# A two-block transformer layer: projections from three float32r matmuls on halves to one plain float32 matmul, and weights laid out in DRAM slot by slot

## The chip, the cores and the metric

The kernel runs on one core of one Trainium2 chip. The metric is the device time of one execution in microseconds (us). TensorE (PE in the profile, with its weight loads as PEld), VectorE (DVE), ScalarE (ACT) and GpSimd (POOL) each have their own instruction stream; SyncE (SP) here only issues DMAs. The streams meet in semaphores, written out by hand.

## The reference, cut to what matters

256 tokens of width 2048 pass through two blocks, all in float32. What the projections compute is plain matrix products with large weights:

```python
mod = c_act @ ada_w + ada_b                      # six vectors of 2048
h = rmsnorm(x, norm1_g) * (1 + sc1) + sh1
z = h @ w_in                                     # q, kc, vc, ks, vs, kw, vw, gates, lx, ly, ga, gb
o_a = nsa_attention(q, kc, vc, ks, vs, kw, vw, gates, ...)   # compressed, selected, window
o_b = gelu(ly) * rg_lru(causal_dwconv(lx), ...)
y = (sigmoid(ga) * (o_a @ proj_a) + sigmoid(gb) * (o_b @ proj_b)) @ w_out
x = x + g1 * y
gate, val = split(h2 @ ffn_up)                   # width 6144 each
x = x + g2 * ((gelu(causal_dwconv(gate)) * val) @ ffn_down)
# second block: another w_in, sliding window attention, s5_ssm, w_glu, w_ssm_proj, w_out
```

## The kernel before, in words

Activations lie transposed: features on the 128 partitions, the 256 tokens along the free axis. The weights are read once. SP walks a fixed list of **slots**, each a load of 1 MB into one of `RAW = 5` buffers `wraw[:, z % RAW, :]` of 2048 float32 a partition. A weight slot is 512 rows by 512 columns of a matrix, taken as four runs of 512 elements (2 KB) a partition. An "ada" slot is 128 rows of `ada_w` transposed (8 KB in one run a partition); VectorE multiplies it by the activated `c` and sums (L1051), which gives one column of `mod`. SP reloads a buffer when its last user is done: `ada_done` for an ada slot, `pe_units` for a weight slot.

A weight slot holds two **units** of 1024 elements a partition, and there are 809 units, in groups (`groups()`): 8 units for a group of 512 output columns of a 2048-row matrix, 12 or 4 for others. Three modes: "T" (weights stationary, 128x128, the activations of 256 tokens moving; all but 25 units), "N" and "TN" (the value projections, activations stationary), and one unit "GATES".

Products are made from halves. A float32 number is cut into a float32r part and the rest. For each unit u, ScalarE copies the raw weights to float32r, `whi` (`split_act`, L1069), and VectorE subtracts it from the raw ones, `wlo`, over the raw buffer (`split_dve`, L1074). Both run `LEAD = 5` units ahead of TensorE, with `HI = 6` buffers `whi`. Activations are cut the same way by `split()` (L308: a cast and a subtraction) into pairs `_hi`, `_lo`. TensorE then issues, for each 128x128 block of weights, three float32r matmuls (L1525): whi by x_hi, whi by x_lo, wlo by x_hi. A T unit is 8 blocks, so 24 matmuls. Groups accumulate in two PSUM buffers (`pairs`, four rows of 256 tokens) in turn.

All engines walk the same order, `walk`: unit by unit, and after each unit some steps of **jobs**. A job is a generator, such as `evac` (read a finished group out of PSUM), `compress`, `nsa` (one of four key-value groups of the first attention; 27 steps), `lru`, `attention2`, `ssm` (eight, 17 steps each) or `norm1`, `norm2` and `last_norms`. Each job is spread over a stretch of units, so that TensorE does a unit, then its part of the next steps, waiting there where an engine has not delivered. The small matmuls of the jobs are plain float32 (into `bank`). The four `nsa` jobs lie in q(1), q(2), q(3), and the last in lx(0) and ly(0), 8 units each for the first three and 16 for the last. Each `ssm` job lies in 10 units of ga2, pa2 and gs2. Because the splits run 5 units ahead and in each engine's own stream, a `whi` that waits for its load or for a free buffer also holds up every ScalarE step behind it.

The start (`prologue`) is four blocks: 8 ada slots, then the norm of four chunks of `h1` (L335, L340, and the split at L310 and L312), then the splits of units 2b and 2b+1. TensorE may run units 2b and 2b+1 once block b of `h1` is there.

The result of the first block is kept in `res`; it goes to DRAM and comes back (`spilled`, `xf_back`, `x_back`) when its place is used for other data.

Of the kernel before, what the change touches and what calls it, by code (L numbers as in the profile page):

```python
# [6 lines left out]
F32 = mybir.dt.float32  # L7
F32R = mybir.dt.float32r
ACT = mybir.ActivationFunctionType
ALU = mybir.AluOpType  # L10
# [12 lines left out]
RAW = 5  # L23
HI = 6
LEAD = 5
# [76 lines left out]
def build_program(nc, ctx, xT, vecs, cvec, W, small, outT):  # L102
# [9 lines left out]
    def put_pair(name, at, n):  # L112
        return put(name + "_hi", at, [P, n, T], F32R), put(name + "_lo", at + n * 1024, [P, n, T], F32R)

# [3 lines left out]
    z0, z1, z2, rM, rW = 0, 32 * K, 64 * K, 96 * K, 112 * K  # L118
    rWh = rW + RAW * 8 * K
    rC = rWh + HI * 4 * K  # L120
    rT = rC + 8 * K
    rS = rT + 8 * K
    h1, m1 = put_pair("h1", z0, DC), put_pair("m1", z0, DC)
    oa, ob = put_pair("oa", z1, DC), put_pair("ob", z2, DC)
    h2, h3, m2 = put_pair("h2", z2, DC), put_pair("h3", z2, DC), put_pair("m2", z2, DC)
    hid = put_pair("hid", z0, 24)
    res = put("res", rM, [P, DC, T])
    wraw = put("wraw", rW, [P, RAW, 2048])
    wlo = put("wlo", rW, [P, RAW, 2, 1024], F32R)
    whi = put("whi", rWh, [P, HI, 1024], F32R)  # L130
# [3 lines left out]

    k2 = put("k2", z2, [P, 2, 4, T])
# [22 lines left out]
    u_2 = put("u_2", z1, [P, 8, T])  # L158
    q_2 = put("q_2", z1 + 8 * K, [P, 8, T])
    ag_2 = put("ag_2", z1 + 16 * K, [P, 8, T])  # L160
    k_2 = put("k_2", z1 + 24 * K, [P, 2, T])
    v_2 = put("v_2", z1 + 28 * K, [P, 2, T])
    rs2 = put("rs2", z1 + 30 * K, [P, 2, T])
    z_2 = put("z_2", z0, [P, 8, T])
    at_ = put_pair("at", z0 + 8 * K, 8)
    gs_2 = put("gs_2", z0 + 8 * K, [P, DC, T])
    y_2 = put("y_2", z1 + 24 * K, [P, 8, T])
    ys = put_pair("ys", z2, 8)
    sg = (put("sg_hi", z1, [P, 8, T], F32R), put("sg_lo", z1 + 24 * K, [P, 8, T], F32R))
    mg2 = put("mg2", z1 + 8 * K, [P, DC, T])  # L170
# [6 lines left out]
    ph = put("ph", z0 + 24 * K, [P, 4, 32, 16])  # L177
# [35 lines left out]
    def sem(name):  # L213
# [3 lines left out]
    hi_ready, lo_ready, pe_units, ada_done = sem("hi_ready"), sem("lo_ready"), sem("pe_units"), sem("ada_done")  # L217
# [3 lines left out]
    wcmp_in, wgate_in, x_back, spilled, ssm_in, xf_back = (sem("wcmp_in"), sem("wgate_in"), sem("x_back"),  # L221
                                                           sem("xf_spilled"), sem("ssm_in"), sem("xf_back"))
# [5 lines left out]
    X = {"h1": h1, "m1": m1, "h2": h2, "h3": h3, "m2": m2, "oa": oa, "ob": ob, "hid0": hid, "hid1": hid, "at": at_,  # L228
         "ys": ys, "sg": sg}
    block = ctx.enter_context(nc.Block())  # L230

    GR, of = groups()
    U0, U1 = [], []
    at = 0
    for gr in GR:
        U0.append(at)
        at += gr.units
        U1.append(at)
    N_UNITS = at
    SLOTS, HEAD = [], []  # L240
    unit_slot = {}
    behind = {}
    for g, gr in enumerate(GR):
        for s in range(gr.slots):
            per = gr.units // gr.slots
            if g == 0:
                HEAD.append(range(len(SLOTS), len(SLOTS) + 8))
                SLOTS += [("ada", col + c) for c in range(4 * s, 4 * s + 4) for col in (16, 0)]
            for n in range(per):
                unit_slot[U0[g] + s * per + n] = (len(SLOTS), n)  # L250
            SLOTS.append(("w", g, s, U0[g] + (s + 1) * per))
            for col in gr.ada.get(s, ()):
                behind.setdefault(U0[g] + (s + 1) * per - 1, []).append(len(SLOTS))
                SLOTS.append(("ada", col))
    N_ADA = 0
    ada_no = {}
    for z, slot in enumerate(SLOTS):
        if slot[0] == "ada":
            ada_no[z] = N_ADA
            N_ADA += 1  # L260
    where = []
    for gr in GR:
        where += [(gr, n) for n in range(gr.units)]
# [44 lines left out]
    def split(dst, at, n, src):  # L308
        hi, lo = dst
        ve.tensor_copy(hi[:, at:at + n, :], src)  # L310
        ve.drain()
        return ve.tensor_tensor(lo[:, at:at + n, :], src, hi[:, at:at + n, :].bitcast(F32), ALU.subtract)  # L312

# [15 lines left out]
    def normed(j, name, dst, c, r, gain, shift=None):  # L329

        me, ins = j.me, None
        if me == "dve":
            tt = (t1, t2)[c // 4 % 2]
            for n in range(4):
                ve.scalar_tensor_tensor(out=tt[:, n, :], in0=res[:, c + n, :], scalar=gain[:, c + n:c + n + 1], in1=r,  # L335
                                        op0=ALU.mult, op1=ALU.mult)
            ve.drain()
            if shift is not None:
                for n in range(4):
                    ve.tensor_scalar(tt[:, n, :], tt[:, n, :], mod[:, shift + c + n:shift + c + n + 1], None, ALU.add)  # L340
                ve.drain()
            ins = split(dst, c, 4, tt[:, :, :])
        j.ready[name].append(j.give("to_pe", "dve", ins))
# [69 lines left out]
    def nsa(j, i):  # L413
# [116 lines left out]
        for hd in range(4):  # L530
# [42 lines left out]
            if me == "dve":  # L573
                ins = split(oa, i * 4 + hd, 1, bank[3][:, 0:1, :])
                ve.drain()
# [3 lines left out]
    def lru(j, i):  # L579
# [59 lines left out]
        if me == "dve":  # L639
            ve.tensor_tensor(lr[:, :, :], lr[:, :, :], t2[:, :, :], ALU.mult)  # L640
            ve.drain()
            ins = split(ob, i * 4, 4, lr[:, :, :])
# [48 lines left out]
    def attention2(j, pair, e):  # L691
# [60 lines left out]
        for hd in range(4):  # L752
# [37 lines left out]
            if hd % 2:  # L790
                c = g * 2 + hd // 2
                if me == "dve":
                    j.eng.wait_ge(*evacuated("ag2", c // 4))
                if me == "dve":
                    ve.tensor_tensor(t1[:, 0:1, :], bank[3][:, 0:1, :], ag_2[:, c:c + 1, :], ALU.mult)
                    ve.drain()
                    split(at_, c, 1, t1[:, 0:1, :])
                    ve.drain()
# [20 lines left out]
    def ssm_tables(j):  # L819
# [4 lines left out]
        if me == "dve":  # L824
            j.eng.wait_ge(spilled, 16)
            ins = ve.drain()
        yield from j.hand("to_act", "dve", "act", ins)
# [233 lines left out]
    def width(u):  # L1061
        return 768 if where[u][0].mode == "GATES" else 1024

    def split_act(act, u):
        (z, half), r, w = unit_slot[u], u % HI, width(u)
        act.wait_ge(w_loaded[z % RAW], 16 * (z // RAW + 1))
        if u >= HI:
            act.wait_ge(pe_units, u - HI + 1)
        sc.activation(whi[:, r, 0:w], wraw[:, z % RAW, 1024 * half:1024 * half + w], ACT.Copy).then_inc(hi_ready, 1)  # L1069

    def split_dve(dve, u):
        (z, half), r, w = unit_slot[u], u % HI, width(u)
        dve.wait_ge(hi_ready, u + 1)
        ve.tensor_tensor(wlo[:, z % RAW, half, 0:w], wraw[:, z % RAW, 1024 * half:1024 * half + w],  # L1074
                         whi[:, r, 0:w].bitcast(F32), ALU.subtract).then_inc(lo_ready, 1)
        for z in behind.get(u, ()):
            ada(dve, z)

    def split_unit(j, u):
        if j.me == "act":  # L1080
            split_act(j.eng, u)
        if j.me == "dve":
            split_dve(j.eng, u)

    FIRST = 8

    def prologue(j):
# [17 lines left out]
        for b in range(4):  # L1105
# [12 lines left out]
            split_unit(j, 2 * b)  # L1118
            split_unit(j, 2 * b + 1)

    def merged(j):

        me, ins = j.me, None
        for b in range(3):
            if me == "dve":
                if b == 0:
                    j.eng.wait_ge(pe_units, U1[of("gb", 3)])
                ins = split(m1, 4 * b, 4, res[:, 4 * b:4 * b + 4, :])
            j.ready["m1"].append(j.give("to_pe", "dve", ins))
            yield  # L1130

    def evac(j, g):
# [54 lines left out]
        elif k == "pa":  # L1187
            if me == "dve":
                j.eng.wait_ge(*evacuated("ga", i))
            if computed("dve"):  # L1190
                done(ve.tensor_tensor(rows(res), t1[:, :, :], e[:, :, :], ALU.mult))
                ve.drain()
        elif k == "pb":
            if me == "dve":
                j.eng.wait_ge(*evacuated("gb", i))
            if computed("dve"):
                done(ve.tensor_tensor(t2[:, :, :], t2[:, :, :], e[:, :, :], ALU.mult))
                ve.drain()
                ve.tensor_tensor(rows(res), rows(res), t2[:, :, :], ALU.add)
                ve.drain()  # L1200
            if i == 3:
                if me == "dve":
                    ins = split(m1, 12, 4, rows(res))
                j.ready["m1"].append(j.give("to_pe", "dve", ins))
                j.sync("to_pool", "dve", "pool", j.drained())
                if me == "pool":
                    po.dma_start(res[:, :, :], xT.rearrange("(c p) t -> p c t", p=P)).then_inc(x_back, 16)
        elif k in ("wout", "down"):
            g0 = 32 if k == "wout" else 80
            if k == "wout" and i == 0 and me == "dve":  # L1210
                eng.wait_ge(x_back, 16)
# [412 lines left out]
```

## Time and profile before

| | us |
|---|---|
| median of 3 runs | 3039.63 (3038.92 to 3040.29) |
| the profiled execution, its time | 3035.36 |
| its span, first to last instruction | 3033.6 |
| PE busy | 2647.2 (87%), 20558 matmul records |
| DVE busy | 1913.4 (63%) |
| ACT busy | 1126.1 (37%) |
| mean granted clock of TensorE | 0.932 |

Busy means that at least one instruction of the engine was in flight. Matmuls overlap in the pipeline, so the mean of one (293 ns for the commonest) is far longer than the time from one to the next. The granted clock has two levels, 1.2 and 2.4 GHz, shown as 0.5 and 1.0; a figure between is a mean over time. A plain float32 matmul leaves two records of a matmul and two of a weight load, a float32r one leaves one of each.

### The profile page before, as it was taken

What the parts mean: (1) busy time and instruction counts of PE and PEld (TensorE: products, weight loads), DVE (VectorE), ACT (ScalarE), POOL (GpSimd) and SP (SyncE); (2) the same over time, 40 slices, a digit from 0 to 9 for tenths busy, and PEclk for the clock granted to TensorE, in tenths of its full rate; (3) what the DMA queues carried; (4) which work ended last, traced back from release to release, by engine and by line L of the source; (5) the groups of instructions that cost most, each with busy time, mean ns of one, the idle gap of its engine ahead of it and who ended that gap; (6) DMA issues with size and microseconds to landing.
All of it is one profiled execution on the core that took longest, in us unless ns stands there. A gap on an engine that the chain in (4) does not pass through costs nothing.

```text
span 3033.6 us, 48120 instructions
## 1 busy us (share of the span) xinstructions
PE 2647.2 (87%) x20558; PEld 2570.9 (85%) x20558; DVE 1913.4 (63%) x2538; ACT 1126.1 (37%) x1423; POOL 164.1 (5%) x141
## 2 busy tenths in 40 slices
PE   2499766899999999899999999998898866667899
PEld 2489665899999999899999999998887756666899
DVE  7855444666766565677554555545876687777663
ACT  1122222456533334243443444443444322323332
POOL 0000000000000000000000000000000233332000
PEclk7689888999999999899999999999999978878899
DMA  8765322345677776477555555544543323333454
GB/s 350 279 230 209 129 84 84 125 148 180 235 271 270 280 267 230 156 275 277 197 185 186 183 181 181 183 166 138 177 143 122 119 91 101 104 101 115 153 176 144
DMA packets 237990, 548.20 MB, mean 181 GB/s; under 512 B 10672, under 2 KB 14768, under 8 KB 225360
## 3 DMA queue, kind: packets, MB, share of 16 engines
q1 hardware_dynamic: 233664, 530.31, 50.5%
q0 software_dynamic: 4112, 14.81, 1.4%
q8 instruction: 162, 2.65, 0.3%
q14 instruction: 52, 0.43, 0.0%
HBM read 540.89 MB, written 4.19 MB: 180 GB/s over the span
## 4 chain that ended last, share of the span: by engine, by line
PE 75%; DVE 14%; DVEq 4%; DMA 4%; ACT 2%; issue 2%; PEldq 0%; PEld 0%; ACTq 0%
PE pair L1525 67%; DVE wlo L1074 3%; DMA wraw<-ada_wT_dram 2%; DVE wraw L1051 2%; DMA wraw<-w_in_dram 1%; DVEq L809 1%; PE pair L1531 1%; ACT whi L1069 1%; DVE ssb L812 1%; DVE ssb L810 1%; DVE ssb L815 1%; DVEq L814 1%; PE bank L390 1%; PE bank L566 1%; DVE ssb L808 1%
## 5 line engine op out<-in xcount | busy, mean ns | idle before, releaser
L1074 DVE TENSOR_TENSOR wlo<-wraw,whi 128x1024 fp32r<-128x1024 f32 x809 | 997.7, 1245 | 874.2 <-ACT whi L1069 852.0
L1069 ACT ACTIVATE whi<-wraw 128x1024 fp32r<-128x1024 f32 x809 | 844.5, 1057 | 1632.9 <-PE pair L1525 950.4
L1525 PE MATMUL pair<-h_hi,whi 128*128 128x256 f32 x4128 | 1208.0, 293 | 171.1 <-DVE wlo L1074 90.3
L1525 PE MATMUL pair<-h_lo,whi 128*128 128x256 f32 x4128 | 1192.8, 289 | 0.0
L1525 PE MATMUL pair<-h_hi,wlo 128*128 128x256 f32 x4128 | 1190.6, 288 | 0.0
L1525 PEld LDWEIGHTS pair<-h_hi,whi 128*128 128x128 f32 x4128 | 818.9, 198 | 190.5 <-issue 117.6
L1525 PEld LDWEIGHTS pair<-h_lo,whi 128*128 128x128 f32 x4128 | 819.1, 198 | 0.5
L1525 PEld LDWEIGHTS pair<-h_hi,wlo 128*128 128x128 f32 x4128 | 817.5, 198 | 0.0
L1051 DVE SCALAR_TENSOR_TENSOR wraw<-wraw,cb 128x2048 f32<-128x2048 f32 x96 | 218.7, 2287 | 28.8 <-DMA wraw<-ada_wT_dram 27.7
L1525 PE MATMUL pair<-hid_hi,whi 128*128 128x256 f32 x768 | 218.5, 284 | 0.0
L1525 PE MATMUL pair<-hid_lo,whi 128*128 128x256 f32 x768 | 217.3, 283 | 0.0
L1525 PE MATMUL pair<-hid_hi,wlo 128*128 128x256 f32 x768 | 217.3, 283 | 0.0
L1525 PEld LDWEIGHTS pair<-hid_lo,whi 128*128 128x128 f32 x768 | 147.4, 192 | 0.2
L1525 PEld LDWEIGHTS pair<-hid_hi,whi 128*128 128x128 f32 x768 | 147.4, 192 | 0.2
L1525 PEld LDWEIGHTS pair<-hid_hi,wlo 128*128 128x128 f32 x768 | 147.4, 192 | 0.0
L1525 PE MATMUL pair<-m_hi,whi 128*128 128x256 f32 x512 | 145.5, 284 | 0.0
L1525 PE MATMUL pair<-m_lo,whi 128*128 128x256 f32 x512 | 144.9, 283 | 0.0
L1525 PE MATMUL pair<-m_hi,wlo 128*128 128x256 f32 x512 | 144.9, 283 | 0.0
L1525 PEld LDWEIGHTS pair<-m_lo,whi 128*128 128x128 f32 x512 | 98.3, 192 | 0.1
L1525 PEld LDWEIGHTS pair<-m_hi,whi 128*128 128x128 f32 x512 | 98.3, 192 | 0.1
L1525 PEld LDWEIGHTS pair<-m_hi,wlo 128*128 128x128 f32 x512 | 98.3, 192 | 0.0
L1525 PE MATMUL pair<-oa_hi,whi 128*128 128x256 f32 x256 | 72.4, 283 | 0.0
(391 smaller groups left out, 3131.5 us busy)
## 6 DMA issues: line engine op xcount, KB each, us to landing
wraw<-w_in_dram SPq DMA_DIRECT2D x172, 1024.0 KB, 5.2
wraw<-ada_wT_dram SPq DMA_DIRECT2D x96, 1024.0 KB, 5.3
wraw<-ffn_up_dram SPq DMA_DIRECT2D x96, 1024.0 KB, 5.0
wraw<-ffn_down_dram SPq DMA_DIRECT2D x48, 1024.0 KB, 5.0
wraw<-w_out_dram SPq DMA_DIRECT2D x32, 1024.0 KB, 5.1
wraw<-proj_a_dram SPq DMA_DIRECT2D x16, 1024.0 KB, 6.8
wraw<-proj_b_dram SPq DMA_DIRECT2D x16, 1024.0 KB, 6.2
wraw<-w_attn_proj_dram SPq DMA_DIRECT2D x8, 1024.0 KB, 5.0
```

The lines of the kernel that those rows point to most:

```text
L390: ins = te.matmul(bank[1][:, 0, 0:60], wcmp[:, l, :], blocks[:, l, :], start=(l == 0), stop=(l == 31))
L566: te.matmul(bank[3][:, 0, :], vv(br, 0), pt[:, br, 0:T], start=False, stop=False, skip_group_check=True)
L808: en.tensor_tensor(y, a_im, b_im, ALU.mult)
L809: en.drain()
L810: en.tensor_tensor(o_re, x, y, ALU.add if conj else ALU.subtract)
L812: en.tensor_tensor(x, a_re, b_im, ALU.mult)
L814: en.drain()
L815: last = en.tensor_tensor(o_im, x, y, ALU.subtract if conj else ALU.add)
L1051: ve.scalar_tensor_tensor(out=wraw[:, slot, :], in0=wraw[:, slot, :], scalar=1.0, in1=cb[:, :], op0=ALU.mult, op1=ALU.mult, accum_out=mod[ ...
L1069: sc.activation(whi[:, r, 0:w], wraw[:, z % RAW, 1024 * half:1024 * half + w], ACT.Copy).then_inc(hi_ready, 1)
L1074: ve.tensor_tensor(wlo[:, z % RAW, half, 0:w], wraw[:, z % RAW, 1024 * half:1024 * half + w], whi[:, r, 0:w].bitcast(F32), ALU.subtract).t ...
L1525: ins = te.matmul(pair[:, o, :], w[:, at_w + o * P:at_w + (o + 1) * P], x, start=(k == 0 and o % 2 == 0 and t == 0), stop=(k == last and t ...
```

## The change: what it does

1. Projections take the raw weights from `wraw` and plain float32 activations; one matmul replaces three. `split`, `split_act`, `split_dve`, `split_unit`, `LEAD`, `HI`, the buffers `whi` and `wlo` and the `_hi`/`_lo` pairs go.
2. TensorE waits on the slot's load itself (`w_loaded`), once a slot. Ada slots are now handled on VectorE at their place in the unit order rather than 5 units earlier.
3. The freed SBUF goes to weight buffers: `RAW` from 5 to 9, and to separate places for `m1` and the second block's data, so that `res` is never moved out and back: its three DMAs and their waits go, and the job `merged` with them.
4. On the host the weights are copied into one DRAM array `stream`, in the order of the slots, each laid out as it will lie in SBUF, so that every load is one run of 8 KB a partition.

```diff
-RAW = 5
-HI = 6
-LEAD = 5
+RAW = 9
...
     def normed(j, name, dst, c, r, gain, shift=None):
...
-            ins = split(dst, c, 4, tt[:, :, :])
...
-    def split_act(act, u):
-        (z, half), r, w = unit_slot[u], u % HI, width(u)
-        act.wait_ge(w_loaded[z % RAW], 16 * (z // RAW + 1))
-        if u >= HI:
-            act.wait_ge(pe_units, u - HI + 1)
-        sc.activation(whi[:, r, 0:w], wraw[:, z % RAW, 1024 * half:1024 * half + w], ACT.Copy).then_inc(hi_ready, 1)
-
-    def split_dve(dve, u):
-        (z, half), r, w = unit_slot[u], u % HI, width(u)
-        dve.wait_ge(hi_ready, u + 1)
-        ve.tensor_tensor(wlo[:, z % RAW, half, 0:w], wraw[:, z % RAW, 1024 * half:1024 * half + w],
-                         whi[:, r, 0:w].bitcast(F32), ALU.subtract).then_inc(lo_ready, 1)
...
-            gr, s = GR[slot[1]], slot[2]
...
-                src = W[gr.w][4 * P * s:4 * P * (s + 1), gr.col:gr.col + CB].rearrange("(k p) n -> p k n", p=P)
-                dst = wraw[:, z % RAW, :].rearrange("p (k n) -> p k n", k=4)
-            sp.dma_start(dst, src).then_inc(w_loaded[z % RAW], 16)
+            n = DC * 48 if slot[0] == "w" and GR[slot[1]].mode == "GATES" else 2048
+            sp.dma_start(wraw[:, z % RAW, 0:n], stream[z, :, 0:n]).then_inc(w_loaded[z % RAW], 16)
...
         def unit(g, gr, u, n):
-            if FIRST <= u + LEAD < N_UNITS:
-                split_dve(dve, u + LEAD)
+            for z in behind.get(u, ()):
+                ada(dve, z)
...
-            pe.wait_ge(lo_ready, u + 1)
-            wh, wl = whi[:, r, :], wlo[:, z % RAW, half, :]
-            terms = lambda k: ((wh, hi[:, k, :]), (wh, lo[:, k, :]), (wl, hi[:, k, :]))
+            if half == 0:
+                pe.wait_ge(w_loaded[z % RAW], 16 * (z // RAW + 1))
+            w = wraw[:, z % RAW, 1024 * half:]
...
                     for o in range(4 if gr.mode == "T" else 2):
-                        for t, (w, x) in enumerate(terms(k)):
-                            ins = te.matmul(pair[:, o, :], w[:, at_w + o * P:at_w + (o + 1) * P], x,
-                                            start=(k == 0 and o % 2 == 0 and t == 0), stop=(k == last and t == 2),
-                                            skip_group_check=True)
+                        ins = te.matmul(pair[:, o, :], w[:, at_w + o * P:at_w + (o + 1) * P], x[:, k, :],
+                                        start=(k == 0 and o % 2 == 0), stop=(k == last), skip_group_check=True)
```

The jobs' own arithmetic, their steps and their places in the unit order are as before.

## Rows read from the trace of the kernel before

**Rows 1.** The page: busy by engine, granted clock by fortieths, chain's shares.
```profile
PE 2647.2 (87%) x20558; PEld 2570.9 (85%) x20558; DVE 1913.4 (63%) x2538; ACT 1126.1 (37%) x1423; POOL 164.1 (5%) x141
...
PEclk7689888999999999899999999999999978878899
...
PE 75%; DVE 14%; DVEq 4%; DMA 4%; ACT 2%; issue 2%; PEldq 0%; PEld 0%; ACTq 0%
```

**Rows 2.** Stretches: length, busy (x instructions) by engine, clock, DMA share, GB/s.
```profile
0.00:141.10 141.10, 40.34 (x225) 38.20 (x226) 115.29 (x162) 23.58 (x24) 3.05 (x14) 0.69 0.80 322
141.10:299.70 158.60, 151.88 (x1004) 142.74 (x1003) 88.06 (x131) 43.41 (x44) 6.15 (x6) 0.92 0.61 219
299.70:625.20 325.50, 244.84 (x1634) 226.99 (x1634) 161.05 (x341) 102.64 (x228) 0.00 (x0) 0.87 0.30 104
625.20:1169.10 543.90, 543.90 (x4482) 542.12 (x4482) 366.89 (x352) 255.69 (x293) 5.62 (x7) 1.00 0.70 246
1169.10:1284.30 115.20, 103.00 (x803) 100.94 (x802) 68.41 (x94) 38.49 (x37) 0.00 (x0) 0.93 0.46 157
1284.30:2025.00 740.70, 740.70 (x6163) 740.28 (x6162) 427.16 (x439) 306.51 (x323) 0.00 (x0) 1.00 0.60 204
2025.00:2115.50 90.50, 79.89 (x627) 78.12 (x625) 40.89 (x47) 36.29 (x42) 0.00 (x0) 0.99 0.46 152
2115.50:2403.80 288.30, 259.00 (x1924) 242.48 (x1924) 209.62 (x471) 119.27 (x189) 1.17 (x1) 0.95 0.42 136
2403.80:2839.30 435.50, 296.94 (x2178) 272.78 (x2177) 331.91 (x410) 135.75 (x178) 148.16 (x113) 0.82 0.32 104
2839.30:3033.60 194.30, 186.68 (x1536) 186.27 (x1536) 104.15 (x95) 64.50 (x66) 0.00 (x0) 0.98 0.50 168
```

**Rows 3.** Groups of instructions: count, busy, mean ns, idle before and its releaser.
```profile
L1074 DVE TENSOR_TENSOR wlo<-wraw,whi 128x1024 fp32r<-128x1024 f32 x809 | 997.7, 1245 | 874.2 <-ACT whi L1069 852.0
L1069 ACT ACTIVATE whi<-wraw 128x1024 fp32r<-128x1024 f32 x809 | 844.5, 1057 | 1632.9 <-PE pair L1525 950.4
```

**Rows 4.** A job's float32 matmuls amid projections: timeline (start, length) and line's durations.
```profile
633.87 3.62 PE L590 MATMUL bank<-t,wgate 128*128 128x256 f32 x16
...
L590 PE MATMUL bank<-t,wgate x64: 377/379/483, 633.9 to 785.9; 128*128 128x256 f32 x64
```

**Rows 5.** VectorE in the third block of the start; then DMA GB/s by fortieths.
```profile
86.92 2.29 DVE L1051 SCALAR_TENSOR_TENSOR wraw<-wraw,cb 128x2048 f32<-128x2048 f32 x1 [3.28 <-DMA wraw<-ada_wT_dram]
...
97.48 1.67 DVE L335 SCALAR_TENSOR_TENSOR t<-res,scA,rstd 128x256 f32<-128x256 f32 x4
99.23 1.14 DVE L340 TENSOR_SCALAR t<-t,mod 128x256 f32<-128x256 f32 x4
100.45 0.69 DVE L310 CAST h_hi<-t 128x1024 fp32r<-128x1024 f32 x1
101.22 1.22 DVE L312 TENSOR_TENSOR h_lo<-t,h_hi 128x1024 fp32r<-128x1024 f32 x1
102.36 2.35 DVE L1074 TENSOR_TENSOR wlo<-wraw,whi 128x1024 fp32r<-128x1024 f32 x2
...
GB/s 121 374 366 425 435 418 432 423 415 426 428 428 170 0 0 330 425 425 417 428 428 230 0 119 421 428 406 431 435 421 21 0 286 430 423 398 409 408 323 5
```

**Rows 6.** Waits (total, times, longest), 299.7 to 625.2 us; then one head's steps.
```profile
ACT whi L1069 <- DMA wraw<-w_in_dram: 60.8, 9, 9.7
...
440.73 1.01 DVE L514 TENSOR_SCALAR sm<-sm,st 128x128 f32<-128x128 f32 x4
...
443.37 0.87 ACT L552 ACTIVATE pt<-bank 128x384 f32<-128x384 f32 x2 [4.30 <-PE bank L548]
```

**Rows 7.** Wait, 2403.8 to 2839.3 us; then VectorE's timeline, two complex products.
```profile
PE pair L1525 <- DVEq L302: 74.5, 8, 11.4
...
2476.90 0.69 DVE L807 TENSOR_TENSOR ssb<-ssb,ssb 128x512 f32<-128x512 f32 x1 [0.16 <-issue]
...
2493.72 1.76 DVE L807 TENSOR_TENSOR ssb<-t,ssb 128x512 f32<-128x512 f32 x1
```

More of the change, by code:

```diff
@@ L99, in groups, with schedule, build_program @@
     return out, of
-def build_program(nc, ctx, xT, vecs, cvec, W, small, outT):
+def schedule():
+    GR, of = groups()
+    U0, U1 = [], []
+    at = 0
+    for gr in GR:
+        U0.append(at)
+        at += gr.units
+        U1.append(at)
+    SLOTS, HEAD = [], []
+    unit_slot = {}
+    behind = {}
+    for g, gr in enumerate(GR):
+        for s in range(gr.slots):
+            per = gr.units // gr.slots
+            if g == 0:
+                HEAD.append(range(len(SLOTS), len(SLOTS) + 8))
+                SLOTS += [("ada", col + c) for c in range(4 * s, 4 * s + 4) for col in (16, 0)]
+            for n in range(per):
+                unit_slot[U0[g] + s * per + n] = (len(SLOTS), n)
+            SLOTS.append(("w", g, s, U0[g] + (s + 1) * per))
+            for col in gr.ada.get(s, ()):
+                behind.setdefault(U0[g] + (s + 1) * per - 1, []).append(len(SLOTS))
+                SLOTS.append(("ada", col))
+    N_ADA = 0
+    ada_no = {}
+    for z, slot in enumerate(SLOTS):
+        if slot[0] == "ada":
+            ada_no[z] = N_ADA
+            N_ADA += 1
+    return GR, of, U0, U1, SLOTS, HEAD, unit_slot, behind, ada_no
+def build_program(nc, ctx, xT, vecs, cvec, stream, small, outT):
     base = 16640
@@ L226, in build_program @@
         S[key] = sem(key)
-    X = {"h1": h1, "m1": m1, "h2": h2, "h3": h3, "m2": m2, "oa": oa, "ob": ob, "hid0": hid, "hid1": hid, "at": at_,
-         "ys": ys, "sg": sg}
+    X = {"h1": h1, "m1": m1, "h2": h2, "h3": h3, "m2": mg2, "oa": oa, "ob": ob, "hid0": hid, "hid1": hid, "at": at_,
+         "ys": y_2, "sg": sg}
     block = ctx.enter_context(nc.Block())
[L232 to L263, printed above, removed]
+    GR, of, U0, U1, SLOTS, HEAD, unit_slot, behind, ada_no = schedule()
+    N_UNITS = U1[-1]
     def evacuated(kind, i):
@@ L823, in ssm_tables @@
         ins = None
[L824 to L827, printed above, removed]
+        yield from j.hand("to_act", "dve", "act", j.drained())
         if me == "act":
@@ L1190, in evac @@
             if computed("dve"):
[L1191 removed]
+                done(ve.tensor_tensor(rows(m1), t1[:, :, :], e[:, :, :], ALU.mult))
                 ve.drain()
@@ L1198, in evac @@
                 ve.drain()
-                ve.tensor_tensor(rows(res), rows(res), t2[:, :, :], ALU.add)
+                ins = ve.tensor_tensor(rows(m1), rows(m1), t2[:, :, :], ALU.add)
+            j.ready["m1"].append(j.give("to_pe", "dve", ins))
+            if me == "dve":
                 ve.drain()
[L1201 to L1207, printed above, removed]
         elif k in ("wout", "down"):
             g0 = 32 if k == "wout" else 80
-            if k == "wout" and i == 0 and me == "dve":
-                eng.wait_ge(x_back, 16)
             if computed("dve"):
@@ L1468, in _ @@
         prologue(j)
-        def unit(g, gr, u, n):
-            if FIRST <= u + LEAD < N_UNITS:
-                split_act(act, u + LEAD)
-        walk(j, unit)
+        walk(j, nothing)
     @block.vector
@@ L1501, in unit @@
         def unit(g, gr, u, n):
-            r, (z, half) = u % HI, unit_slot[u]
-            pair, last = pairs[g % 2], 2 * gr.units - 1
-            hi, lo = X[gr.x]
+            z, half = unit_slot[u]
+            pair, last, x = pairs[g % 2], 2 * gr.units - 1, X[gr.x]
             if n == 0 and g >= 2:
@@ L1620 @@
     with ExitStack() as ctx:
-        build_program(nc, ctx, xT, vecs, cvec, W, small, outT)
+        build_program(nc, ctx, xT, vecs, cvec, stream, small, outT)
     r = run(nc, [arrays], core_ids=[0])
```

184 lines of the change are left out of this document (60 added, 124 removed).

## The prediction

> **What bounds the kernel now.** I read the page first. TensorE is busy 87% of the span and makes 75% of the chain of waits; VectorE's 63% and ScalarE's 37% are lower, and the granted clock is full in the long middle and 0.7 to 0.8 at the start and late [rows 1]. Then I cut the span into stretches whose ends are group boundaries, found by counting 24 matmul records a unit [rows 2]. Two kinds appear. From 625 to 1169 and from 1284 to 2025 us TensorE never idles, at full clock: 256 units take 740.7 us less two sums of squares of 1.73 us, 2.88 us a unit, 0.120 us a float32r matmul. Elsewhere (nsa from 300 to 625, the ssm jobs from 2404 to 2839, the start) TensorE waits and its clock falls with it. VectorE and ScalarE lead the table of groups with the weight splits, 998 and 845 us, but these mostly waited themselves for TensorE to free a buffer [rows 3]: the splits bound nothing in the full stretches. So what a projection matmul costs on TensorE decides two thirds of the time, and what the splits get in the way of decides the rest.
>
> **The price of a plain float32 matmul.** The trace has it, in the shape that the change uses. Eight matmuls of job `lru`, 128x128 weights, other weights each time, 256 tokens moving, stand between projection units as 16 records. They run from 633.87 for 3.62 us, and one record lasts 0.38, so the 15 intervals are 3.24 us: 0.216 us a record, 0.432 us a matmul [rows 4]. Three float32r matmuls are 0.360. A T unit goes from 2.88 to 8 x 0.432 = 3.456 us, +0.576 us. For the 16 N units (512 tokens wide, half as many) I take the same; the one GATES unit falls by some 4 us (32 short matmuls for 96). On TensorE alone, 808 units cost +465 us.
>
> **Full stretches.** 625 to 1169: 184 units, 543.9 + 106.0 = 649.9. 1284 to 2025: 740.7 + 147.5 = 888.2. The last stretch, 64 units: 194.3 + 36.9, less some 2.5 us of splits between groups = 228.7. The passages with a norm, 32 and 24 units: 115.2 + 18.4 and 90.5 + 13.8. Of their bubbles one cast and one subtraction of the first block go, 0.69 + 1.22 [rows 5], some 2 us each: 131.6 and 102.3. DMA is no bound: the hungrier of the two moves 246 GB/s now, with its engines at 0.70 [rows 2], and longer units ask for less.
>
> **The start (141.1 us).** Per block, VectorE does 8 ada products of 2.29 us (18.3), the norm (1.67 + 1.14 and 0.8 of small ones), the split (0.69 + 1.22) and two weight splits (2.35), and stands 3.3 us or more for a load, after DMA holes of zero between plateaus of 425 GB/s [rows 5]. A block is 29.7 us now. The splits go. With nine buffers the holes close: 9 loads at 1.05 MB and 425 GB/s are 22.2 us, VectorE's own 18.3 + 3.6 = 21.9. The first block of `h1` is there at some 41 us, by the same terms; three more at 22 give 107; units 6 and 7, partly at the lower clock, 9: the ninth unit starts at 116, 25 us earlier. If the holes stay, 7 us a block, the gain is about 10.
>
> **kv and compress (141 to 300).** 40 units at 2.88, GATES 11.5 and two sequences of 64 short records, 14.7 together, are 141.4; 17 us are waits, most for loads that come late behind the compress weights. After: 138.2 + 7.4 + 14.7 and 5 of waits = 165, against 158.6.
>
> **nsa (300 to 625).** 48 units are 138.2 us. One nsa job puts some 17.4 us of its own on TensorE, an estimate from the rate above: per head 1792 columns of scores and values at 0.432/256, and transposes and the compressed part, 5. Four are 69.6. The remaining 325.5 - 207.8 = 118 us are waiting and slow clock. In 60.8 us of it ScalarE's next `whi` stood waiting for a load, with the job's softmax copies queued behind it [rows 6]: the queue moves, not the arithmetic. After the change ScalarE has nothing but the jobs, and nine buffers cover the loads. What remains is the job's chain. Per head TensorE waits for the weights of the softmax (1.01 us of scalings [rows 6] and small operations before, some 2.3) and for ScalarE's copies (0.87 [rows 6], some 1.1). 27 steps on 8 units put one unit of 3.46 us in every 3.4 steps, which covers about one of the two. Four heads leave about 7 us, the ten steps before them 5. So 12 us for each of three jobs, 4 for the fourth, on 16 units: 165.9 + 69.6 + 40 = 275.5, 50 less than now. Bounds: all waits gone, 235; the 118 kept, 353. I stay nearer to the low end, since the load waits that lead now have no place left.
>
> **Second block's front (2115.5 to 2403.8).** 72 units are 207.4, jobs 30, waits 51. The wait for `res` to reach DRAM goes, and VectorE, busy 209.6 of 288.3 us [rows 2], is rid of 72 x 1.25 = 90. After: 248.8 + 30 + 24 (half of the waits) = 303, +15. Bounds 279 and 330.
>
> **ssm (2403.8 to 2839.3).** 80 units are 230.4 us, the jobs' own matmuls 3.1 each; 180 us are waits and slow clock (0.82), of which 74.5 in 8 waits at L1525 for a drained VectorE [rows 2, 7]. VectorE is busy 332 of 435 us, 80 x 1.43 = 115 of it `wlo`: here the split is in the chain. Without it, one half of a job is two complex products of six operations at 0.69 us and the scans, 4.3 + 2.4 + 4.2 = 10.9 us. TensorE has four units (13.8 us) to do before it asks for the first half and three (10.4) before the second. GpSimd's products lengthen one of VectorE's from 0.69 to 1.76 at the start of a clash [rows 7]; by the rows around it a clash costs 3.5 us a job. I take 5.3 us of waiting a job: 276.5 + 24.8 + 43 = 344, 91 less. Bounds: none left, 301; the 180 kept, 481. The nearest rows are VectorE's own durations, which are unchanged, so I take the value near the low end.
>
> On that clash the Trainium skill, "SBUF — State Buffer" (section "Who interferes with whom"), says that a VectorE instruction with two SBUF inputs and a reading GpSimd one exclude each other for a whole instruction. The trace agrees in kind (1.76 for 0.69). By that rule GpSimd's products could all fall into VectorE's new gaps, and the stage would be 8 x 3.5 = 28 us shorter.
>
> **The sum.** 116 + 165 + 275.5 + 649.9 + 131.6 + 888.2 + 102.3 + 303 + 344 + 228.7 = 3204 us of span, against 3033.6: matmuls +465, waits -294. The profiled execution's time was 1.8 us above its span, and the median 4.3 above that: 3210 us, +5.6%.
>
> The layout in runs of 8 KB I price at nothing beside the start: ada loads, in 8 KB runs, and w_in loads, in 2 KB runs, both go on the plateaus near 425 GB/s [rows 5], and nowhere else does DMA bound. If that cover is wrong it can only help in the start, where it is counted.
>
> **Rivals.** (1) The waits don't shrink: they belong to the chains of dependent steps, not to splits and loads. For: each hand-over remains, and at the lower clock a float32 matmul costs 0.864. Against: `whi` waiting for loads leads the nsa stretch, `wlo` is a third of VectorE's work in ssm. Half of my gains there lost: 50/2 + 68/2 for nsa (waits 118 to 79) and ssm (180 to 112), 39 + 69 and 14 elsewhere, some 3330; all lost, 3460. (2) Everything hides: 40, 43, 24 and 10 us of remaining waits go: 3093 + 6, about 3100. Against: dependent hand-overs can't all be covered. (3) Faster than before: the spacing in a long stream of float32 matmuls is shorter than in the 16 records, where the change of kind cost something at either end. To break even it must be 0.432 - 171/6464 = 0.405 us a matmul, 0.203 a record; at 0.120 a record, the float32r spacing, the projections take 1.92 us a unit and the kernel would end near 2500, if the loads kept up. Against: one record lasts 377 to 379 ns in nearly all of 64 [rows 4], which leaves no room for a mixture of spacings.
>
> A rule of the Trainium skill would have it so: "TensorE: Matmul & The Clock Gate", section "Back-to-back issue gap", gives some 131 ns a matmul for sustained streams of 512 columns; with two passes of 256 a record that would be 0.26 us a float32 matmul, an estimate from that page, and a kernel faster than before. The 0.216 us a record says otherwise.
>
> **How the numbers follow.** Forecast 0.72, its own range 3150 to 3280 (nsa 255 to 310, ssm 320 to 385, the start 116 to 131). Rival 1: 0.16. Rival 2: 0.08. Rival 3: 0.03; 0.01 for a loss so small that it can't be told from none. The range reaches halfway into rivals 1 and 2: 3135 to 3310. A change of 0.2% (6 us) is about what a measurement of this kernel can tell from none. Faster 0.03, same 0.01, slower 0.96.
>
> **What would show it.** Right: projection records 0.216 us apart and eight-unit groups 27.6 us apart in the middle (23.0 now), clock 1.00; the stretch answering to 1284-2025 at 888 us; the ninth unit at about 116; the nsa stretch near 275 and ssm near 344, with ScalarE near 280 us busy and VectorE near 870. Wrong: another spacing; TensorE in nsa or ssm waiting as long as now; TensorE idle before L1525 for a load after the start; ssm bound by GpSimd.

## The result, and the profile after

The changed kernel takes 3214.88 us (median of 4 runs, 3210.68 to 3215.65), against 3039.84 before: ratio 1.0573, 95% interval 1.0555 to 1.0592. Forecast were 3210 us and a range of 3135 to 3310. The profiled execution took 3210.68 us, its span is 3209.0.

The page after: busy by engine, then the granted clock by fortieths, the chain's shares by engine, and the costliest group with its idle time.

```profile
span 3209.0 us, 32617 instructions
...
PE 3047.5 (95%) x14126; PEld 2610.1 (81%) x14126; DVE 851.7 (27%) x1617; ACT 292.4 (9%) x614; POOL 139.1 (4%) x138
...
PEclk7899999999999999999999999999999999999999
...
PE 88%; DVE 7%; DVEq 2%; DMA 1%; issue 1%; ACT 1%; SPq 0%; PEldq 0%; POOLq 0%; POOL 0%; PEld 0%; ACTq 0%
...
L1417 PE MATMUL pair<-h,wraw 128*128 128x256 f32 x8256 | 1841.7, 384 | 92.8 <-DVE h L329 60.5
```

Against [rows 1], TensorE is busy 400 us more in a span 175 us longer, and VectorE and ScalarE have lost 1062 and 834 us. The commonest matmul is now L1417 in plain float32, two records each.

The same ten stretches, cut at the same group boundaries as [rows 2] (the ends are read to within about 2 us); the columns are the same.

```profile
0.00:114.80 114.80, 46.76 (x158) 37.91 (x159) 91.76 (x141) 11.90 (x12) 3.05 (x14) 0.75 1.00 415
114.80:277.40 162.60, 162.60 (x720) 121.33 (x719) 43.39 (x92) 0.77 (x3) 6.20 (x6) 0.99 0.59 226
277.40:551.40 274.00, 250.65 (x1251) 210.98 (x1250) 95.93 (x277) 54.04 (x180) 0.00 (x0) 0.98 0.34 124
551.40:1200.60 649.20, 649.20 (x3009) 571.51 (x3008) 136.97 (x152) 69.84 (x109) 4.46 (x6) 1.00 0.54 203
1200.60:1331.50 130.90, 122.19 (x548) 106.14 (x547) 23.99 (x54) 6.55 (x8) 0.00 (x0) 0.95 0.38 137
1331.50:2219.00 887.50, 887.50 (x4114) 781.28 (x4113) 95.03 (x159) 39.16 (x65) 0.00 (x0) 1.00 0.47 170
2219.00:2322.20 103.20, 94.66 (x434) 82.57 (x433) 10.87 (x25) 11.15 (x18) 0.00 (x0) 0.99 0.38 133
2322.20:2622.60 300.40, 291.44 (x1349) 242.32 (x1348) 113.41 (x376) 45.04 (x118) 0.00 (x0) 0.99 0.35 123
2622.60:2984.70 362.10, 322.81 (x1541) 263.00 (x1540) 219.89 (x324) 49.77 (x95) 125.34 (x112) 0.95 0.34 122
2984.70:3209.00 224.30, 219.69 (x1018) 193.04 (x1017) 20.43 (x22) 4.20 (x10) 0.00 (x0) 1.00 0.34 122
```

| stretch | before | forecast | after |
|---|---|---|---|
| start, to the ninth unit | 141.1 | 116 | 114.8 |
| kv and compress | 158.6 | 165 | 162.6 |
| nsa | 325.5 | 275.5 | 274.0 |
| full, lx(1) to wout(0) | 543.9 | 649.9 | 649.2 |
| passage with norm2 | 115.2 | 131.6 | 130.9 |
| full, the feed-forward part | 740.7 | 888.2 | 887.5 |
| passage with the last norms | 90.5 | 102.3 | 103.2 |
| second block's front | 288.3 | 303 | 300.4 |
| ssm | 435.5 | 344 | 362.1 |
| end | 194.3 | 228.7 | 224.3 |

The spacing stands in the timeline (start, length, count) of the feed-forward part: 38 intervals in 8.58 - 0.38 = 8.20 us are 0.216 us a record, as in [rows 4].

```profile
1599.75 8.58 PE L1417 MATMUL pair<-h,wraw 128*128 128x256 f32 x39
```

### The profile page after: what moved, and what is told of

It reads as the page before. It is cut to its first block, busy times and chain, and to the rows that moved or that the text cites. A ratio compares the mean times of both kernels' runs of the same rounds, so it can differ in the third digit from the quotient of the medians.

```text
span 3209.0 us, 32617 instructions
## 1 busy us (share of the span) xinstructions
PE 3047.5 (95%) x14126; PEld 2610.1 (81%) x14126; DVE 851.7 (27%) x1617; ACT 292.4 (9%) x614; POOL 139.1 (4%) x138
## 3 DMA queue, kind: packets, MB, share of 16 engines
q1 hardware_dynamic: 76608, 530.31, 44.6%
## 4 chain that ended last, share of the span: by engine, by line
PE 88%; DVE 7%; DVEq 2%; DMA 1%; issue 1%; ACT 1%; SPq 0%; PEldq 0%; POOLq 0%; POOL 0%; PEld 0%; ACTq 0%
PE pair L1417 80%; DVE wraw L1031 2%; PE pair L1421 2%; DVE ssb L795 1%; DVE ssb L793 1%; DVEq L792 1%; DMA wraw<-stream_dram 1%; DVE ssb L790 1%; DVE ssb L798 1%; DVEq L797 1%; DVE ssb L961 1%; PE bank L553 1%; PE bank L315 0%; PE pair L1425 0%; PE bank L377 0%
## 5 line engine op out<-in xcount | busy, mean ns | idle before, releaser
L1417 PE MATMUL pair<-h,wraw 128*128 128x256 f32 x8256 | 1841.7, 384 | 92.8 <-DVE h L329 60.5
L1417 PEld LDWEIGHTS pair<-h,wraw 128*128 128x128 f32 x8256 | 1583.7, 193 | 329.1 <-issue 43.1
L1417 PE MATMUL pair<-hid,wraw 128*128 128x256 f32 x1536 | 332.8, 379 | 0.0
L1417 PEld LDWEIGHTS pair<-hid,wraw 128*128 128x128 f32 x1536 | 291.8, 190 | 39.7
L1417 PE MATMUL pair<-oa,wraw 128*128 128x256 f32 x512 | 111.2, 379 | 0.0
L1417 PE MATMUL pair<-m,wraw 128*128 128x256 f32 x512 | 111.2, 379 | 0.0
L1417 PE MATMUL pair<-ob,wraw 128*128 128x256 f32 x512 | 111.2, 379 | 0.0
L1417 PE MATMUL pair<-mg,wraw 128*128 128x256 f32 x512 | 110.7, 379 | 0.0
L1417 PEld LDWEIGHTS pair<-oa,wraw 128*128 128x128 f32 x512 | 97.3, 190 | 13.2
L1417 PEld LDWEIGHTS pair<-m,wraw 128*128 128x128 f32 x512 | 97.3, 190 | 13.2
L1417 PEld LDWEIGHTS pair<-mg,wraw 128*128 128x128 f32 x512 | 97.3, 190 | 13.2
L1417 PEld LDWEIGHTS pair<-ob,wraw 128*128 128x128 f32 x512 | 97.3, 190 | 13.2
L1417 PE MATMUL pair<-at,wraw 128*128 128x256 f32 x256 | 57.3, 381 | 2.4 <-DVEq L297 2.4
L1417 PEld LDWEIGHTS pair<-at,wraw 128*128 128x128 f32 x256 | 48.1, 190 | 11.0 <-DVEq L297 2.8
L1417 PE MATMUL pair<-u,wraw 128*128 128x256 f32 x256 | 55.4, 379 | 0.0
```

Of the source, the lines that this page charges most:

```text
L1417: ins = te.matmul(pair[:, o, :], w[:, at_w + o * P:at_w + (o + 1) * P], x[:, k, :], start=(k == 0 and o % 2 == 0), stop=(k == last), skip_ ...
```

## The experiments

Stretches below are cut at the same units as above. "nsa" and "ssm" are the third and the ninth. A span is that of the profiled execution, some 1.7 us below its time. The kernels of experiments 4, 8 and 9 leave out work that the result needs; they price it and are no candidates.

**1. The old layout in the changed kernel** (`e1_old_layout`)

```diff
-            sp.dma_start(wraw[:, z % RAW, 0:n], stream[z, :, 0:n])...
+                src = stream[gr.w][4 * P * s:4 * P * (s + 1), gr.col:gr.col + CB].rearrange("(k p) n -> p k n", p=P)
+                dst = wraw[:, z % RAW, :].rearrange("p (k n) -> p k n", k=4)
+            sp.dma_start(dst, src)...
```

> The changed kernel with the old layout in DRAM: weight loads again in runs of 2 KB a partition, nine buffers kept. My theory (the layout is worth nothing where a load is hidden): 3215 us, within 0.2%, the ninth unit within 2 us of 114.8. Rival (short runs load slower, and the start or the dense ga/gb stretch feels it): the load takes a higher DMA share for the same bytes, and the time is 3225 or more.

3215.95 us, ratio to before 1.0584 (1.0568 to 1.06), which overlaps the changed kernel's. The ninth unit starts at 114.0. The full stretch is as long to 0.1 us, and only the DMA share (next to last column) differs, 0.58 for 0.54 at the same 203 GB/s:

```profile
553.60:1202.90 649.30, 649.30 (x3010) 571.57 (x3010) 137.06 (x152) 69.84 (x109) 4.46 (x6) 1.00 0.58 203
```

The rival's first half came true and its second did not: short runs do keep the DMA engines busier for the same bytes (weight queue 47.7% of the span for 44.6%), and it costs nothing. They also load somewhat slower. From 100 to 120 us, where the loads are mostly of `w_in` and back to back, the last column is 410 GB/s in this kernel, in runs of 2 KB, and 427 in the changed one, in runs of 8 KB:

```profile
100.00:120.00 20.00, 14.41 (x57) 12.39 (x58) 9.93 (x30) 0.00 (x0) 2.48 (x2) 0.75 1.05 410
```

```profile
100.00:120.00 20.00, 14.38 (x54) 12.15 (x55) 9.26 (x26) 0.00 (x0) 2.47 (x2) 0.72 1.01 427
```

**2. Five weight buffers in the changed kernel** (`e2_five_buffers`)

```diff
-RAW = 9
+RAW = 5
```

> The changed kernel with 5 weight buffers for 9. If the buffers close the holes of the start, as predicted, the ninth unit moves from 114.8 to 135 or so, and the holes at 7 us a block are back: 3235. In nsa the theory that splits queued behind loads were the trouble says 5 buffers are nearly enough without them: 274 to 285. Rival (depth alone cured the waits for loads): nsa goes back above 310 and the time to 3270 or more.

3231.27 us, ratio 1.0637 (1.0621 to 1.0653). The ninth unit starts at 132.4 for 114.8, and that is all but a microsecond of the difference (spans 3227.5 and 3209.0): nsa is 273.7, as with nine, and ssm is as long too. The holes are back. DMA GB/s by fortieths of the start, first of the changed kernel, then of this one; before it was [rows 5]:

```profile
GB/s 60 381 380 394 446 417 434 425 417 440 422 417 442 420 428 431 422 431 420 411 434 425 431 425 422 425 425 428 425 431 422 431 428 428 428 431 422 422 428 428
```

```profile
GB/s 92 380 383 424 426 428 423 428 428 426 426 428 428 57 0 109 418 431 423 423 428 433 191 42 376 426 423 428 426 433 297 0 314 411 431 428 421 428 413 7
```

**3. The new layout in the kernel before** (`e3_before_stream`)

```diff
-                src = W[gr.w][4 * P * s:4 * P * (s + 1), gr.col:gr.col + CB].rearrange("(k p) n -> p k n", p=P)
-                dst = wraw[:, z % RAW, :].rearrange("p (k n) -> p k n", k=4)
-            sp.dma_start(dst, src)...
+            sp.dma_start(wraw[:, z % RAW, 0:n], W[z, :, 0:n])...
```

> The kernel before with the new DRAM layout alone. My theory: no change, 3040 within 0.2%, since ada loads had 8 KB runs and the others were hidden or waited on a buffer to come free, not on bandwidth. Rival: 1% faster, with the waits of whi for loads (60.8 us in the nsa stretch) shrinking.

3046.19 us, ratio 1.0016 (1.0003 to 1.0029): no gain. The loss, 6 us, is of the size that I had called just measurable, and the interval just excludes no change. The profiled execution is 10 us longer in the kv stretch (168.7) and within 1.2 us elsewhere; whether that is the layout or this execution isn't settled.

**4. The weight splits left out from the ninth unit on, all else as before** (`e4_no_splits`)

```diff
 def split_act(act, u):
+    if u >= FIRST:
+        return
...
+                wl = whi[:, (r + 1) % HI, :]
+                if half == 0:
+                    pe.wait_ge(w_loaded[z % RAW], 16 * (z // RAW + 1))
```

> The kernel before with the weight splits left out from the ninth unit on: TensorE issues its three float32r matmuls a block from halves made once, and waits for each slot's load itself; five buffers, loads in 2 KB runs and all else as before (the projections' numbers are left out of account). It parts the two terms of the sum. My theory: full stretches stay at 2.88 us a unit (625 to 1169 in 544 us, 1284 to 2025 in 741), nsa falls from 325 to some 250, ssm from 435 to some 330, the whole to 2850. Rival 1 of the prediction (waits belong to the chains): nsa above 290, ssm above 385, the whole above 2930.

2849.8 us, ratio 0.9382 (0.9368 to 0.9396). This is the experiment that parts the sum. nsa, the two full stretches and ssm:

```profile
286.80:550.90 264.10, 231.13 (x1635) 214.99 (x1635) 104.97 (x294) 53.73 (x180) 0.00 (x0) 0.94 0.38 129
550.90:1095.00 544.10, 544.10 (x4486) 542.43 (x4485) 152.87 (x170) 69.93 (x109) 5.62 (x7) 1.00 0.70 246
1209.00:1951.90 742.90, 742.90 (x6181) 742.48 (x6180) 118.29 (x185) 41.01 (x68) 0.00 (x0) 1.00 0.60 204
2307.20:2663.70 356.50, 282.02 (x2163) 262.98 (x2162) 221.98 (x323) 49.45 (x94) 123.84 (x109) 0.88 0.39 129
```

The full stretches don't move (the feed-forward part is 740.7 us from its first unit's first record, this window ends 2 us later): there the splits were hidden, 974 us of VectorE's and ScalarE's busy time in these two stretches alone ([rows 2] less these rows). nsa loses 61 us and ssm 79, somewhat less than the 75 and 105 expected, but beyond the bounds set for the rival. The kv stretch loses 15 (143.6 for 158.6) and the second block's front 29 (259.7 for 288.3). In nsa and ssm the changed kernel is within 10 and 6 us of these lengths although its units cost 20% more. So most of what the change gains in waits, 184 us, comes with the splits' going, and its loss is the price of the matmul.

**5 and 6. The kernel before with its splits nearer** (`e5_lead3`, `e11_lead2`)

```diff
-LEAD = 5
+LEAD = 3        # 2 in the second
```

> The kernel before with the splits 3 units ahead for 5, nothing else. The last run put 61 us of the nsa stretch and 79 of ssm on the splits. If the trouble in nsa is that a split stands too far ahead in ScalarE's queue, waiting for a load that itself waits for TensorE to free a buffer, then 3 ahead frees it: nsa 325 to 290 or less, ssm nearly as before (there it is VectorE's work, which stays), full stretches as they are, the whole 3000. Rival (it is the splits' work, not their place): nsa above 315 and the whole within 0.5% of before.

2971.41 us, ratio 0.9779 (0.975 to 0.9808). nsa 282.6, ssm 420.9, the full stretches unchanged.

> The kernel before with the splits 2 units ahead. Dose and response for the place of the splits: if only waiting behind late loads mattered, 2 ahead is at least as good as 3 in nsa (283 or less) and the whole 2960 to 2975. If the lead also has to cover the splits' own 2.3 us and the jobs' long VectorE steps, TensorE now waits for wlo in the full stretches or in ssm, and the whole is above 2985.

2973.5 us, ratio 0.978 (0.9766 to 0.9795), the same as with 3. nsa 278.1, ssm 421.2; the passages and the second block's front, 292.3, give most of the gain back. The rival, TensorE waiting for `wlo` in the full stretches or in ssm, did not show. Below 3 there is no more to have. The wait that goes (total, times, longest; nsa stretch; 5 ahead is [rows 6], 60.8), first 3 ahead, then 2:

```profile
ACT whi L1069 <- DMA wraw<-w_in_dram: 24.2, 6, 9.5
```

```profile
ACT whi L1069 <- DMA wraw<-w_in_dram: 12.9, 3, 9.4
```

In nsa most of the harm was the place of the splits and not their work: 43 of the 61 us that leaving them out brings come from one constant. In ssm the place is worth 15 of 79; the rest goes only with the splits themselves. `LEAD` moves VectorE's splits along with ScalarE's, so these runs don't say in which of the two queues the harm was done.

**7. Six raw buffers, four for the halves, 3 ahead** (`e6_lead3_six`)

```diff
-RAW, HI, LEAD = 5, 6, 5
+RAW, HI, LEAD = 6, 4, 3
```

> The same with 6 raw buffers and 4 for whi (same SBUF). If loads are still late at 3 ahead, one more buffer helps: 5 to 15 us below the run before it, in the start and in nsa. Rival (place alone mattered): the same time within 0.3%, or slower where only 4 whi buffers hold ScalarE back.

2990.88 us, ratio 0.9854 (0.9834 to 0.9874), slower than with 5 and 6. The start and the kv stretch gain 15 us (135.7 and 144.6 for 141.9 and 153.0), nsa loses 3, the second block's front 7 and ssm 15. The rival held: by the pages of the two profiles ScalarE's splits stood 1316 us waiting for TensorE's units (545 with five and six buffers), which fits it. The edit changes both numbers at once, so what each is worth is not parted.

**8. GpSimd's products left out in seven of the eight jobs** (`e7_no_clash`)

```diff
-                ins = cmul(f4(E[q2][0]), ...
+                if m:
+                    ins = po.drain()
+                else:
+                    ins = cmul(f4(E[q2][0]), ...
```

> The changed kernel with GpSimd's products for the state phases left out for 7 of the 8 ssm jobs (their numbers are stale, all waits kept). It prices the clash of GpSimd with VectorE in the changed kernel: by the trace VectorE's product at the second half of a job takes 7.9 us for 4.3. Theory (TensorE waits for exactly that product): ssm falls from 362 by 7 x 3.6 = 25, to 337, and the mean of the slow products to 0.69 us each. Rival (the lengthening falls in time that VectorE would have waited for TensorE anyway): less than 8 us.

3182.36 us, ratio 1.0478 (1.0455 to 1.05). ssm is 331.1 for 362.1, 31 us less, more than the 25 expected:

```profile
2625.90:2957.00 331.10, 311.48 (x1545) 255.61 (x1544) 196.43 (x324) 50.57 (x96) 24.21 (x28) 0.99 0.38 134
```

VectorE has the same 324 instructions and is busy 23 us less. TensorE's idle time falls from 39.3 to 19.6 us (length less PE busy), and the granted clock rises from 0.95 to 0.99: part of the gain is clock. VectorE's waits for GpSimd's results, which go as well, were 1.4 us in all. The clash itself, from VectorE's timeline in the changed kernel; the second row is the same line on the same shapes 10 us later, in the product behind the scans, when GpSimd is idle (its products run from 2694.5 to 2702.9 and again from 2711.1):

```profile
2697.05 1.75 DVE L791 TENSOR_TENSOR ssb<-t,ssb 128x512 f32<-128x512 f32 x1
...
2707.36 0.68 DVE L791 TENSOR_TENSOR ssb<-t,ssb 128x512 f32<-128x512 f32 x1
```

**9. Half of the projection matmuls** (`e8_half_k`)

```diff
-            for kk in range(0 if gr.mode == "GATES" else 2):
+            for kk in range(0 if gr.mode == "GATES" else 1):
```

> The changed kernel with every second 128-row piece of each projection left out: half of the projection matmuls, the same loads, jobs and waits. Theory (TensorE's price a matmul sets the full stretches and nothing is close below): a unit falls from 3.456 to 1.73 us, 1.8 us less a unit in the full stretches: 649 to 331 + some, 887 to 447, unless loads bind; a slot every 3.46 us asks for 303 GB/s, with ada slots 450, so the stretch with ada slots (ga, gb) is held at 2.5 us a slot, some 350. nsa and ssm shrink by less than half of what their units lose (nsa to 215 or more, ssm to 290 or more), since the chains come out. The whole near 2000. Rival (chains already bound nsa and ssm in the changed kernel): these two don't move at all.

2004.87 us in one run. nsa, the full stretch with ada slots, the feed-forward part, ssm:

```profile
228.10:445.40 217.30, 184.22 (x866) 147.52 (x867) 95.69 (x277) 54.54 (x180) 0.00 (x0) 0.90 0.43 156
445.40:781.20 335.80, 334.16 (x1540) 291.63 (x1539) 138.06 (x153) 69.85 (x109) 4.46 (x6) 1.00 0.94 378
856.20:1302.10 445.90, 445.90 (x2068) 392.53 (x2067) 95.97 (x161) 38.95 (x65) 0.00 (x0) 1.00 0.90 339
1559.60:1887.80 328.20, 210.42 (x897) 153.76 (x897) 220.99 (x325) 49.51 (x96) 125.81 (x112) 0.80 0.38 135
```

The feed-forward part halves (887.5 to 445.9): nothing but TensorE is near there, even at 339 GB/s. The stretch with ada slots, where I expected loads to bind at 350, is 335.8, with the DMA engines busy 0.94 at 378 GB/s; taking 1.73 us off each of its 184 units would give 331. Of the 83 us of matmul taken out of nsa's 48 units 57 show in its length. That is within the 215 or more that I had set, but not "less than half of what their units lose". In ssm only 34 of 138 show. Its 8 jobs stop near 41 us each. In the changed kernel they take 45, of which TensorE's own work is 37.7. So ssm is close to bound by the chain of its jobs, which is what the forecast of 344 undervalued.

**10 to 12. Each way where it is better** (`e9_mixed`, `e10_mixed_six`, `e12_mixed_pa2`). The kernel before, splits 3 ahead, but plain float32 in groups of the ssm stretch; `h3` is joined from its halves once.

```diff
+PLAIN = ("ga2", "gs2")          # and "pa2" in the last
...
+                ins = ve.tensor_tensor(h3w[:, 4 * b:4 * b + 4, :], at, lo[:, 4 * b:4 * b + 4, :].bitcast(F32), ALU.add)
...
+                        ins = te.matmul(pair[:, o, :], w[:, kk * CB + o * P:kk * CB + (o + 1) * P], h3w[:, k, :], ...
```

> The kernel before with the splits 3 units ahead, and plain float32 matmuls only in the groups ga2 and gs2 (64 of the 80 units of the ssm stretch): h3's halves are added together once, 4 VectorE additions, and these units take the raw weights without splits. If each way is best where the study puts it (three float32r matmuls where TensorE is full, one float32 where the splits are in the chain), full stretches stay at 2.88 us a unit, nsa at 283, and ssm falls from 421 to 360 (362 in the changed kernel, less 9 for the 16 units that keep three matmuls, with their splits): 2971 - 60 = 2910. Rival (VectorE's remaining splits and GpSimd's clash keep the stretch): ssm above 390, the whole above 2940.

2936.13 us, ratio 0.9654 (0.9638 to 0.9671). ssm 386.7: better than 421 and 27 worse than expected, a little below the rival's bounds.

> The same mixed kernel with 6 raw buffers and 4 for whi. In the run with 3 ahead and 6 buffers the start and the kv stretch gained 15 us and ssm lost 15, where 4 whi buffers held the splits; with no splits in most of ssm that loss should go: 5 to 10 us below the mixed kernel with 5 and 6. Rival: the second block's front, which lost 7, and ssm keep the loss, and both are equal within 0.2%.

2938.97 us, ratio 0.9671 (0.9657 to 0.9686), no gain, as the rival had it. What the start gains (8 us) the second block's front loses (297.6 for 288.1). ssm lost nothing this time (382.4), as expected with few splits left in it.

> The mixed kernel (3 ahead, 5 and 6 buffers) with pa2 in plain float32 too, so that no split is left in the 80 units of the ssm stretch, and the attention's output is kept whole. The mixed kernel's ssm missed by 27 us (387 for 360). If the 16 units of pa2 with their splits made the difference (a split in VectorE's queue between the products, as in the kernel before), ssm now equals the changed kernel's, 362, and the whole falls to 2912. Rival (what the changed kernel has besides, 9 buffers and loads that never wait, or something in how jobs lie there): ssm stays above 380 and the whole above 2930.

2916.79 us, ratio 0.9605 (0.9584 to 0.9625), the fastest of the study, 4% below the kernel before and 9% below the changed one. ssm:

```profile
2351.10:2725.50 374.40, 327.89 (x1544) 266.66 (x1544) 229.68 (x335) 56.74 (x102) 126.47 (x113) 0.94 0.37 121
```

The 16 units with splits explain 12 of the 27 us: the result lies between what was expected (362) and the rival (above 380). It still is 12 above the changed kernel's 362.1, with 46.5 us of idle TensorE for 39.3. Nine buffers are not the cause: the changed kernel with five (experiment 2) has the same ssm, and in none of the three traces does a projection of the stretch wait for a load. Most of the 7 us of idle time is one wait at its end, for halves that are still made of the ssm output, and which the changed kernel doesn't have (total, times, longest):

```profile
PE pair L1568 <- DVE ys_lo L322: 4.8, 1, 4.8
```

The remaining 5 us are in TensorE's busy time (327.9 for 322.8 us, clock 0.94 for 0.95). In this stretch VectorE also joins `h3` and makes the first splits of the next groups, some 1.2 us each; what they cost was not tried.

## Why the prediction was right

**The price.** The step that carries the result, 0.432 us for a plain float32 matmul read from 16 records amid the projections [rows 4], is confirmed in 8256 records of L1417 and more. Both full stretches came within 0.7 us of the sum. Experiment 4 keeps them where they were with the splits gone, and experiment 9 halves the feed-forward one with its matmuls. Shown. Rival 3, a tighter spacing in a long stream, is dead. The Trainium skill, "TensorE: Matmul & The Clock Gate" (section "Back-to-back issue gap"), gives 131 ns a matmul for sustained streams of 512 columns, which I had taken, as an estimate, for a record of two passes of 256. The trace does not agree: it has 216 ns a record.

**The waits.** Forecast at -294 us, they came to 175.4 - 465 = -290. The runs divide them. Splits out of the way: -184 (experiment 4: 2849.2 - 3033.6). Nine buffers for five: -18.5 (experiment 2's span 3227.5 to 3209.0), in the start alone. The remaining -87 were not parted by one edit. 58 of them are in nsa and ssm, where chains hide better under longer units: what is left over units and jobs' own matmuls, waits and slow clock together, falls as the units grow.

| one unit | left in nsa | left in ssm |
|---|---|---|
| 1.73 us (experiment 9) | 65 | 165 |
| 2.88 us (experiment 4) | 56 | 101 |
| 3.46 us (changed kernel) | 38 | 61 |

That it is the length of the unit which does this is argued from the three runs, which differ in more. I had priced this hiding in the nsa and ssm steps (a unit of 3.46 us between two steps) without naming it as a part of its own. Some 13 more are in the start (26.3 and 4.6 of longer units, less the buffers' 17.6). The end of `res`'s moves, to which I gave a part of the 27 us in the second block's front, shows nothing there: experiment 4 keeps the moves, and 22 us are left over units and jobs in it (259.7 - 207.4 - 30) as in the changed kernel (300.4 - 248.8 - 30). Rival 1 fell: half of the gains in nsa and ssm lost would have been 314 and 412.

**The start.** 116 forecast, 114.8 measured. The step rested on nine buffers closing the holes; with five they are back and 17.6 of the 26.3 us are gone. The last 9 come with the splits of weights and activations that go there; no run parts them, since experiment 4 keeps the start as it was.

**nsa.** 275.5 and 274.0. That the place of the splits was the trouble is now shown by `LEAD`; that it was ScalarE's queue rather than VectorE's is argued, from its waits for loads, 60.8, 24.2 and 12.9 us at 5, 3 and 2 ahead. One part was wrong: I wrote that nine buffers would cover the loads. Five do (273.7).

**ssm, the mis-sized term.** 5.3 us of waiting a job were forecast, 7.6 came (362.1 - 276.5 - 24.8 = 60.8 over eight). TensorE's idle time is 39.3 us, 4.9 a job, close to the term. The other 21 are busy time (322.8 us for 276.5 + 24.8 of matmuls), which fits the clock: a mean of 0.95 is a tenth of the stretch, 36 us, at the lower level, and half of that, 18 us, would be lost if TensorE were busy throughout. This is an estimate from the two levels. The step left the clock out, although [rows 2] had shown clock and waits fall together. The clash with GpSimd was priced at 3.5 us a job, 28 us if it went; experiment 8 measured 31 us for seven jobs, 4.4 a job, clock included.

**The exclusion rule.** The Trainium skill, "SBUF — State Buffer" (section "Who interferes with whom"), has a GpSimd product and a VectorE one with two SBUF inputs block each other; the trace agrees again, 1.75 us for 0.68 in the rows of experiment 8. I had cited it as what could shorten ssm if GpSimd's products fell into VectorE's new gaps. They didn't: GpSimd starts its product when VectorE frees its buffer (2694.5 us in the job shown), just before VectorE's next product (2696.0), so the two meet in each job.

**The layout.** Priced at nothing, and nothing was gained in either direction: experiment 1 (taken out of the changed kernel) and 3 (put into the kernel before). The reason given was not quite right: I wrote that both lengths of run go on plateaus near 425 GB/s, and those of 2 KB go at 410 (experiment 1). What held is that no stretch got shorter by it.

**The end** was 224.3 for 228.7: 7 us of waits went (194.3 + 36.9 - 224.3) where I had taken 2.5. Experiment 4, without the weight splits alone, has 190.9 for 194.3, so about half is theirs; the rest may be the halves of the activations, which no run parts.

**How much was luck.** The span missed the sum by 5 us only because misses cancelled: ssm came 18 us above its step, and the nine others together 13 below theirs, the end and the second block's front most. The steps are good to a few microseconds, ssm's to 18.

**Slips of the working.** Rival 1's "50/2 + 68/2" doesn't give the 39 and 69 that were used; these are halves of 78 and 137 us. Rival 2 adds the 6 us from span to median twice: it stood at 3093. The 4 us that GATES loses are matmul and were counted among the waits. None moves the forecast.

## What to carry to other kernels

Where three float32r matmuls on halves replace one float32 matmul, they are cheaper on TensorE (0.360 for 0.432 us here), and the halves cost nothing while TensorE is full; where the other engines' chain leads, the one float32 matmul was the better (ssm 374.4 for 420.9 us). Decide it by stretch of the trace. And before rewriting a pipeline whose helper work runs ahead in the same queue as other steps, try how far ahead it runs: one constant was worth 2.2% here, because an early helper waits for a load that waits for the late consumer.

## What the runs showed that I had not expected

- A plain float32 matmul kept its 0.216 us a record over 256 columns in a stream of thousands, with a new 128x128 weight load (mean 193 ns) hidden under each. A float32r one of the same shape comes every 0.120 us and not in half of 0.216, so the price ratio is 3.6 and not 4: 20% for the exchange of three for one.
- Taking GpSimd's products out of seven jobs shortens a 362 us stretch, in which GpSimd is busy 125 us, by 31; VectorE's 128x512 product goes from 0.68 to 1.75 us.
- DMA in runs of 2 KB moves the same bytes with a share of 0.58 for 0.54 at equal GB/s (203), and its plateau is 410 GB/s for 427, 4% lower.
- Weight buffers beyond five were worth 18 us, all of it in the start: the later stretches did not feel them.
